# Gate rows of the adaptive norms: spread over the partitions by transfers through a line in DRAM instead of by products with diagonals

## The reference, cut to what matters

```
mod = silu(c) @ w_mod + b_mod                 # 6 x 1024, block 1
sh1, sc1, g1, sh2, sc2, g2 = split(mod)
x  = x + g1 * gla_mixer(norm(x)*(1+sc1)+sh1)  # gated linear attention
x  = x + g2 * moe(norm(x)*(1+sc2)+sh2)        # 16 experts, top 2
x  = norm(x) * final_g
for i in 0, 1:                                # block 2, 3 x 1024 each
    shift, scale, gate = split(silu(c2) @ mod_w[i] + mod_b[i])
    x = x + gate * (mix_i(norm(x)*(1+scale)+shift) @ w_out[i])
    # i = 0: MLA and grouped attention, the context is updated
    #        too, with its own gate from c_ctx2
    # i = 1: window attention and a short convolution, x only
```

## Time and profile before

| | |
|---|---|
| three runs | 1036.17, 1036.72 (median), 1038.57 us |
| span of the profiled execution | 1037.2 us (no other time of that execution is given) |
| TensorE busy | 953.9 us, 92%, 4352 records |
| weight loads into TensorE | 510.3 us, 49% |
| VectorE busy | 370.3 us, 36%, 876 records |
| ScalarE busy | 292.4 us, 28%, 679 records |
| POOL busy | 31.0 us, 3%, 53 records |
| DMA | 220.92 MB, mean 213 GB/s |
| the queue that POOL issues to | 2032 packets, 6.84 MB |

### The profile page before, as it was taken

The page is one execution under the profiler, slowest core; times in us unless marked ns, Lnnn a source line. Parts: engine busy times, 40 slices in busy tenths (PEclk is TensorE's granted clock), DMA queues, the critical chain, the costliest instruction groups (busy, mean ns, idle before and its releaser), DMA issues.

```text
span 1037.2 us, 11964 instructions
## 1 busy us (share of the span) xinstructions
PE 953.9 (92%) x4352; PEld 510.3 (49%) x4353; DVE 370.3 (36%) x876; ACT 292.4 (28%) x679; POOL 31.0 (3%) x53
## 2 busy tenths in 40 slices
PE   3899989999999889878877999999999999999998
PEld 1454446546444336323322655576454545676763
DVE  1200597624361000001000350485766423246452
ACT  3210543232322000000000341467666311225330
POOL 0100200000000000000000100000000000000000
PEclk8999999999999999999988999999999999999999
DMA  9955574489569999999999512205644104342411
GB/s 351 357 206 201 97 255 162 171 299 334 212 243 326 376 397 393 397 395 397 396 398 386 191 41 71 82 1 193 213 138 108 34 8 140 112 154 82 134 30 40
DMA packets 100750, 220.92 MB, mean 213 GB/s; under 512 B 2917, under 2 KB 5273, under 8 KB 100553
## 3 DMA queue, kind: packets, MB, share of 16 engines
q1 hardware_dynamic: 95520, 208.54, 55.9%
q0 software_dynamic: 2032, 6.84, 2.5%
q10 hardware_dynamic: 3128, 4.62, 1.2%
HBM read 214.48 MB, written 5.51 MB: 212 GB/s over the span
## 4 chain that ended last, share of the span: by engine, by line
PE 80%; DMA 8%; ACT 4%; SPq 3%; DVE 3%; issue 2%; ACTq 0%; DVEq 0%
PE bank L596 27%; PE bank L863 9%; PE bank L610 9%; DMA arena<-in_w_up_e_dram 5%; PE bank L876 4%; PE bank L893 4%; PE bank L1047 3%; PE bank L1066 3%; PE bank L562 3%; PE bank L888 3%; PE bank L1057 3%; DMA arena<-in_gla_w_in_dram 2%; SPq L1212 2%; PE bank L792 1%; SPq L1207 1%
## 5 line engine op out<-in xcount | busy, mean ns | idle before, releaser
L596 PE MATMUL bank<-arena 128*128 128x512 f32 (+3 forms) x672 | 269.9, 559 | 1.4 <-ACT arena L1443 0.7
L596 PEld LDWEIGHTS bank<-arena 128*128 128x128 f32 x672 | 125.9, 190 | 133.7 <-issue 124.1
L863 PE MATMUL bank<-arena 128*64 128x512 f32 x512 | 120.6, 625 | 13.1 <-issue 13.1
L610 PE MATMUL bank<-arena 128*128 128x256 f32 (+1 forms) x384 | 99.4, 417 | 4.0 <-DMA arena<-in_gla_w_in_dram 2.4
L610 PEld LDWEIGHTS bank<-arena 128*128 128x128 f32 x384 | 72.0, 190 | 32.2 <-issue 21.5
L863 PEld LDWEIGHTS bank<-arena 128*64 128x64 f32 x512 | 43.3, 144 | 87.0 <-issue 86.3
L876 PE MATMUL bank<-arena,con 128*64 128x512 f32 x272 | 62.1, 597 | 9.6 <-ACT con L1535 9.0
L562 PE MATMUL bank<-arena,silu_c 128*32 128x512 f32 x384 | 49.0, 633 | 8.4 <-DMA arena<-in_w_mod_dram 6.0
L1532 ACT ACTIVATE con<-bank 128x256 f32<-128x256 f32 x16 | 6.1, 384 | 177.6 <-PE bank L863 177.6
L2164 DVE TENSOR_TENSOR con<-con,bank 128x256 f32<-128x256 f32 x16 | 6.7, 420 | 135.4 <-ACT con L1532 135.4
L1047 PE MATMUL bank<-arena 64*128 64x512 f32 (+3 forms) x160 | 47.7, 545 | 2.2 <-ACT arena L1705 2.2
(11 more groups left out here) (351 smaller groups left out, 1067.7 us busy)
## 6 DMA issues: line engine op xcount, KB each, us to landing
arena<-in_w_gate_e_dram SPq DMA_DIRECT2D x16, 2048.0 KB, 20.0
arena<-in_w_up_e_dram SPq DMA_DIRECT2D x16, 2048.0 KB, 20.3
arena<-in_w_down_e_dram SPq DMA_DIRECT2D x16, 2048.0 KB, 19.8
arena<-in_w_mod_dram SPq DMA_DIRECT2D x12, 2048.0 KB, 11.8
arena<-in_mod_w_dram SPq DMA_DIRECT2D x12, 2048.0 KB, 8.5
arena<-in_gla_w_in_dram SPq DMA_DIRECT2D x6, 2048.0 KB, 10.8
arena<-in_ab_w_in_dram SPq DMA_DIRECT2D x6, 2048.0 KB, 16.4
arena<-in_cd_w_in_dram SPq DMA_DIRECT2D x6, 2048.0 KB, 7.8
```

The source lines that it names most:

```text
L596: mm = pe.matmul(ps[:, 0:n], lhs[:, k, tile * P:(tile + 1) * P], w[:, k, c0:c0 + n], start=(k == 0), stop=(k == kd_ - 1))
L610: mm = pe.matmul(ps[:, i * n:(i + 1) * n], w[:, k, c * P:(c + 1) * P], rhs[:, k, 0:n], start=(k == 0), stop=(k == KC - 1))
L863: mm = pe.matmul(up_b[64 * j:64 * j + 64, :], h[:, k, :], blocks[:, g + n:u + n + 1:u - g, :], start=(k == 0), stop=(k == KC - 1), tile_po ...
```

## The change

The diagonals, their products and the copies are gone. `gate_row` on POOL's queue takes their place: it writes the gate's columns to a line of 1024 numbers in DRAM, waits until that has landed, and reads the line back into all partitions of the gate's row. VectorE waits for the row's own semaphore where it waited for `gate_bc`. TensorE's wait for the rest of the constants moves from gate 0 to the ranks. The core of the diff:

```
+        gate_lines = nc.dram_tensor("gate_lines", [5, D], F32, kind="Internal").ap()
-        diag_gate, gate_bc, y_added = sem("diag_gate"), sem("gate_broadcast"), sem("y_added")
+        gate_line_out, y_added = [sem(f"gate_line{u}_out") for u in range(5)], sem("y_added")
+        gate_row_in = [sem(f"gate_row{u}_in") for u in range(5)]
...
-            def gate(u):                                     (TensorE)
-                if u == 0:
-                    pe.wait_ge(con_rest_in, 16)
-                pe.wait_ge(diag_gate, u + 1)
...
-                for h in range(2):
-                    ps = banks.open(pe, f"gate{u}_{h}", gate_bc, 2 * u + h + 1)
-                    mm = pe.matmul(ps[:, :], ones, gate_diag[:, 4 * h:4 * h + 4, :], start=True, stop=True)
-                    banks.filled(f"gate{u}_{h}", mm)
...
-            ctx_latents(1)
-            gate(1)
-            ctx_latents(4)
+            ctx_latents(5)
+            pe.wait_ge(con_rest_in, 16)
             pe.wait_ge(routed, 1)
...
-            dve.wait_ge(gate_bc, 2)                          (VectorE)
+            dve.wait_ge(gate_row_in[0], 16)
...
-            dve.wait_ge(gate_bc, 4)
+            dve.wait_ge(gate_row_in[1], 32)
...
-            dve.wait_ge(gate_bc, 8)
+            for u in (2, 3):
+                dve.wait_ge(gate_row_in[u], 16)
...
-            dve.wait_ge(gate_bc, 10)
+            dve.wait_ge(gate_row_in[4], 16)
...
+            def gate_row(u, col, targets):                   (POOL)
+
+                line = gate_lines[u]
+                pool.dma_start(line.rearrange("(k p) -> p k", p=P), col, allow_slow_non_contiguous=True).then_inc(gate_line_out[u], 16)
+                pool.wait_ge(gate_line_out[u], 16)
+                for target, cs in targets:
+                    pool.dma_start(target, line[cs].partition_broadcast(target.shape[0])).then_inc(gate_row_in[u], 16)
+
+            pool.wait_ge(modcol_ready, 6)
+            gate_row(0, mod1[:, 16:24, 0], [(gate_rows[:, 0, :], slice(0, D))])
             banks.wait(pool, "z31")
...
+            pool.wait_ge(o_copied, 4)
+            pool.wait_ge(modcol_ready, 12)
+            gate_row(1, mod1[:, 40:48, 0], [(gate_rows[64 * h:64 * h + 64, 1, 0:512], slice(512 * h, 512 * h + 512))
+                                            for h in range(2)])
             banks.wait(pool, "col17")
...
             pool.dma_start(X[:, 2:4, :], a["ctx_2"][0].rearrange("(t p) d -> p t d", p=P)).then_inc(ctx2_again, 16)
+            pool.wait_ge(modcol_ready, 18)
+            pool.wait_ge(qk_ms, 8)
+            gate_row(2, mod2[:, 0, 16:24, 0], [(gate_rows[:, 0, :], slice(0, D))])
+            gate_row(3, mod2[:, 0, 16:24, 1], [(ctx_gate_row, slice(0, D))])
+            pool.wait_ge(modcol_ready, 24)
+            pool.wait_ge(y_added, 12)
+            gate_row(4, mod2[:, 1, 16:24, 0], [(gate_rows[:, 0, :], slice(0, D))])
```

More of the change, by code:

```diff
@@ L534, in per_unit @@
             return small[:, at + u % 8:at + u % 8 + 1]
-        AB_GATE_AT, AB_OUT_AT = [16, 20], [30]
+        AB_OUT_AT = [30]
         CONV_CHUNKS = [(w, c) for w in ("cd3", "cd4", "cd2") for c in range(4)]
@@ L613, in project_T @@
                 last_use[wname] = name
-            def gate(u):
-                if u == 0:
-                    pe.wait_ge(con_rest_in, 16)
-                pe.wait_ge(diag_gate, u + 1)
-                if u == 1:
-                    ps = banks.open(pe, "gate1_1", gate_bc, 4)
-                    for h in range(2):
-                        mm = pe.matmul(ps[64 * h:64 * h + 64, :], ones[:, 0:64], gate_diag[:, 4 * h:4 * h + 4, :],
-                                       start=True, stop=True, tile_position=(0, 64 * h))
-                    banks.filled("gate1_1", mm)
-                    return
-                for h in range(2):
-                    ps = banks.open(pe, f"gate{u}_{h}", gate_bc, 2 * u + h + 1)
-                    mm = pe.matmul(ps[:, :], ones, gate_diag[:, 4 * h:4 * h + 4, :], start=True, stop=True)
-                    banks.filled(f"gate{u}_{h}", mm)
             pe.wait_ge(con_in, 16)
@@ L768, in _ @@
                     banks.filled(f"oT{t}{g}", mm)
-                if t == 0:
-                    gate(0)
                 pe.wait_ge(oT_ready, 2 * t + 2)
@@ L1107, in ab_between @@
                     mod(18 + m // 4)
-                if m in AB_GATE_AT:
-                    gate(2 + AB_GATE_AT.index(m))
                 if m == 28:
@@ L1155, in _ @@
                 project(f"cdq{t}", "cd0", 0, 512, t, hT, cdq_ready, t + 1)
-            gate(4)
             for g in range(2):
@@ L1326, in turn @@
                     ins.then_inc(turned_a, 1)
-            def gate(u):
-                row = ctx_gate_row if u == 3 else gate_rows[:, u % 2, :]
-                if u == 1:
-                    ps = banks.wait(act, "gate1_1")
-                    act.activation(gate_rows[:, 1, 0:512], ps[:, :], ACT.Copy).then_inc(gate_bc, 2)
-                    return
-                for h in range(2):
-                    ps = banks.wait(act, f"gate{u}_{h}")
-                    act.activation(row[:, 512 * h:512 * h + 512], ps[:, :], ACT.Copy).then_inc(gate_bc, 1)
             act.wait_ge(cols_ready, 2)
@@ L1878, in turn @@
                     ins.then_inc(turned_v, 1)
-            def gate(u, col):
-                if u >= 1:
-                    banks.wait(dve, f"gate{u - 1}_1")
-                dve.tensor_tensor(gate_diag[:, :, :], outer(ident, KC), inner(col, P), ALU.mult).then_inc(diag_gate, 1)
             added = [0]
@@ L2030, in _ @@
             o_copy(1)
-            gate(0, mod1[:, 16:24, 0])
             o_gated(1)
-            dve.wait_ge(gate_bc, 2)
+            dve.wait_ge(gate_row_in[0], 16)
             for t in range(TT):
@@ L2048, in _ @@
                 dve.tensor_copy(parts[32 * j:32 * j + NE, :], ps[32 * j:32 * j + NE, 0:T]).then_inc(parts_copied, 1)
-            gate(1, mod1[:, 40:48, 0])
             score, pick, mask = small_at(32, TT, NE), small_at(64, TT, NE), small_at(96, TT, NE)
@@ L2363, in ab_between @@
                     mod_col(18 + m // 4 - 1)
-                if m + 1 in AB_GATE_AT:
-                    gate(2 + AB_GATE_AT.index(m + 1), mod2[:, 0, 16:24, AB_GATE_AT.index(m + 1)])
                 if m == 28:
@@ L2390, in _ @@
             turn(5, hT, [(0, T, 5)])
-            gate(4, mod2[:, 1, 16:24, 0])
             for n, t in enumerate(CD_TILES):
```

1 line of the change is left out of this document (added).

## The result

The change gains nothing; it is a little slower. The changed kernel has a median of 1039.66 us (16 runs, 1036.60 to 1041.73), the kernel before 1037.38 us (16 runs, 1036.17 to 1038.78); the ratio is 1.0018, with a 95% interval of 1.0010 to 1.0025. Times by that ratio: +1.9 us, +1.0 to +2.6. I had forecast 6.1 us less.

A forecast was written before the change was run, and what follows sets the result against it. TensorE work was taken to bound 80% of the span, with DMA engines nearly full in the expert stage. 0 + 0.5 + 1.7 + 2.2 + 1.7 = 6.1 us off the 1036.7 us median gave 1030.6 us, range 1029 to 1032.5.

The forecast's parts named there:

- The price of a line: On POOL's queue, writing a gate's 1024 numbers to DRAM: taken as 5 us to landing, ends 3.0 and 7.2.
- I cost all of it at 0: POOL's added writes, waits and reads: each row ready long before its use, so 0 us added.
- The tight place: Modulation load issued at 703.58 us, wanted at 720.24: 8.1 us of room, 6.1 us beside it; upper bound costs 1.7.
- Rival (c): At 703.58 us: dear 4-byte writes delay modulation load; slower if a line exceeds 11.6 us, e.g. 1044.3 us; chance 0.14.
- Gate 0: First block's mixer gate: TensorE makes it in a gap while y00 waits for ScalarE, so removal gives 0 us.
- Gate 1: Expert gate, product at 291.63 us: ranks come sooner, 0.5 us gained and carried to the expert stage's end.
- Gates 2 and 3: Second block's layer-one attention loop, at 760.88 and 780.02 us: 1.72 and 2.2 us gained, the latter including a 0.49 us wait.
- Rival (a): Attention, 720 to 826 us: VectorE and ScalarE give half back, 3.4 us gained in all, 1033.3 us; chance 0.17.
- Gate 4: Second block's layer two, at 905.27 us between back-to-back projections: 1.72 us gained.

The follow-up runs named there:

- e4: The changed kernel plus four extra transfers on POOL's idle queue from about 814 us, metering write and read forms, results unread; one run, 1038.61 us.
- e7: The changed kernel plus six extra 4-byte-piece writes to DRAM on POOL from about 608 us, differing in count and spacing; one run, 1038.19 us.
- e6: The kernel before with only the first block's mixer gate made through DRAM, all other gates by products; 1039.66 us, ratio 1.0017 to before.
- e1: The changed kernel with the line writes of the second block's layer-one gates issued at about 608 us, broadcasts unmoved; 1031.33 us, ratio 0.9942 to before.
- e5: e1 with the first block's mixer gate made by the diagonal product again, its transfers removed; 1030.89 us, ratio 0.9937 to before.

## Why the prediction was wrong

**The price of a line** was the step that failed. I bounded it by 3.0 and 7.2 us to landing and took 5, from transfers of 64-byte pieces that are read from DRAM; it measured 11.1 to 14.8. On it hung "I cost all of it at 0, hidden by those distances", and the sign that I had named for being wrong, TensorE waiting for DMA after 700 us, is there with 5.47 us. Both ways in which those rows were near were real (e4: 64-byte pieces written, 1.7 us; 4-byte pieces read, 3.2 us), and the one combination that the change uses was in neither. An estimated 3.5 us of DMA-engine time per line was wrong in kind too: for a part of its time a line takes from a load beside it not its own packets but the load's rate.

**The tight place** was right, and the sum around it too. The room was 8.1 us with a load of 8.5 us; the load took 22.1 us, 13.6 more, and 13.6 - 8.1 = 5.5 us is the wait that TensorE shows (5.47). "Before 704 us the DMA engines are empty, and line 2 lies there" failed with the price: line 2 was under way until 708.5 us, and line 3 until 724. Rival (c) named this mechanism and this place, at 0.14. Its condition (a line over 11.6 us) was met by line 3; the result itself, 0.18% above before, lies in the band within 0.2% that I had at 0.10. Its formula, which lets the load stand still while a line is under way, gives 14.7 + 2.6 - 8.1 = 9.2 us for the wait, more than the 5.5 measured, since the load crept on meanwhile and from 709 to 716 us even ran at full rate. Its price per piece has no meaning (e7).

**The clock** was in none of the terms. Behind the wait at 725 us the granted clock is 0.50, and the stretch up to gate 2's place takes 41.09 instead of 38.73 us: 2.4 us on top of the wait.

**Gate 0** at 0 was half right. y00 starts when ScalarE ends, with the product or without; nothing else comes of its removal at the front. But with the cover that I named, ScalarE's squares and copies, only the time before y00 is covered. What the product did for TensorE itself, keep it at work, I did not ask: without it 1.6 us are lost in the mean behind the gap. The Trainium skill ("TensorE: Matmul & The Clock Gate", Part 1) says that an idle TensorE is set to the lower clock, and that the moment at which this is judged is not tied to the program, so that the same kernel differs from run to run. The table agrees: the same gap of 3.19 us costs 2.90 us in one execution and nothing in another.

**Gate 1**: 0.5 us forecast, 0.55 measured (51.55 against 51.00). Whether it reaches the end of the expert stage the runs don't tell: from the experts' first product to the first projection behind them the eleven executions take 270.3 to 272.0 us. The two with gate 1's product (before 271.84, e6 272.03) are the two longest, the nine without it take 270.3 to 271.7, so the 0.55 us are not given back there. Of the 1.49 us that the changed kernel seems to gain in that stage, 1.0 is the difference of the two means; two executions against nine don't show that it comes from gate 1, and the measured times do not ask for it.

**Gates 2 and 3**: 3.9 forecast, 4.45 measured, the same in after, e1 and e5. The wait of 0.49 us went, nothing took its place, and another half microsecond of small waits went with it. Rival (a), that attention gives half back, is out.

**Gate 4**: 1.72 forecast and found (1.71).

So 6.1 us were forecast for the gates and 6.7 measured; the 0 for the lines missed 6.7 us, and 1.6 us more lay in gate 0.

## What to carry to other kernels

Before a write of single numbers side by side into DRAM goes beside a load that TensorE will want, measure that very form alone, on idle queues, in both directions, and compare it with the same pieces apart; if it is dear, move it to a stretch in which no load runs. When a product is removed from a gap, ask what the gap does to the engine's clock, and not only who ends it. And a profile of one execution shows such a clock loss or doesn't: look at several before a term of 1 to 3 us is put down to an edit.

## What the runs showed of the hardware that I had not expected

- 1024 writes of 4 bytes from 128 partitions into 4 KB of DRAM take 9.4 us on idle DMA engines (11.1 to 14.8 in the changed kernel), 128 of them into 512 bytes 7.5 us; the same 1024 written 512 bytes apart take 3.1 us, read from the 4 KB 3.2 us, and 128 pieces of 64 bytes side by side 1.7 us. For most of a line's time on idle engines the records show a DMA share of 0.00.
- Beside such a line a weight load moves 41 to 42 GB/s at a DMA share of 0.91 to 0.97 for a part of the line's time, and 341 to 362 GB/s in another, earlier part, against some 390 GB/s alone.
- An idle of 3.19 us on TensorE was followed by a spell at the lower clock in six of eight executions, and by 1.00 throughout in two. The kernel before has such a place of its own, behind a stretch with little for TensorE around 712 to 714 us; in e6 the clock stays up there, and that stretch is 1.5 us shorter (146.73 against 148.25). The windows, of before:

```profile
716.00:718.00 2.00, 2.00 (x8) 1.21 (x9) 1.65 (x7) 1.37 (x7) 0.00 (x0) 0.50 0.11 33
```

and of e6:

```profile
716.00:718.00 2.00, 2.00 (x15) 1.14 (x13) 1.90 (x9) 2.00 (x10) 0.00 (x0) 1.00 0.35 127
```

Why the clock falls in one execution and not in the next, and by which part of the write path numbers side by side hinder each other, stays open.
